# Early blocks split one block sooner, their low parts on VectorE, and row operations of the groups in another order

## The reference

```python
s = jnp.einsum('bhpd,phnd->bhpn', q, sub_keys).astype(jnp.float32)
top_s, top_i = lax.top_k(s, PEER_TOPK)
...
eid = e1 * PEER_NKEYS + e2
gate = jax.nn.softmax(best_s, axis=-1)
u_sel = expert_u[eid]
act = jax.nn.gelu(jnp.einsum('bd,bhkd->bhk', xb, u_sel).astype(jnp.float32), approximate=False)
v_sel = expert_v[eid]
return jnp.einsum('bhk,bhkd->bd', (gate * act).astype(xb.dtype), v_sel)
```

## Time and profile before

| | us |
|---|---|
| median of 3 runs | 3806.78 |
| lowest and highest | 3801.97, 3807.18 |
| the profiled execution, its own time | 3811.23 |
| its span | 3809.5 |
| PE busy | 3467.4 (91%) |
| DVE busy | 2623.9 (69%) |
| ACT busy | 1017.8 (27%) |
| POOL busy | 1063.9 (28%) |
| mean granted TensorE clock, share of full | 0.95 |

### The profile page before, as it was taken

One profiled execution on the slowest core, in us unless ns is written; L12 is line 12 of the kernel. 1 busy time (PEld: TensorE's weight loads), 2 busy tenths in 40 slices (PEclk: granted clock), 3 DMA queues, 4 the chain that ended last, 5 costly groups with the idle time before them and its releaser, 6 DMA issues.

```text
span 3809.5 us, 57302 instructions
## 1 busy us (share of the span) xinstructions
PE 3467.4 (91%) x21552; PEld 3385.4 (89%) x21552; DVE 2623.9 (69%) x4889; ACT 1017.8 (27%) x1345; POOL 1063.9 (28%) x809
## 2 busy tenths in 40 slices
PE   6989999899998999886888799999999999999997
PEld 6989999699998999885777789999999999999996
DVE  5553434223443499997666788888888888888886
ACT  5732222111322232222333222222222222222222
POOL 0000000000000233221111545555455555544551
PEclk8999999699999999997888999999999999999998
DMA  2111111111322233224655989888888888888983
GB/s 100 39 36 37 35 44 44 50 44 45 135 84 73 93 116 106 88 92 127 190 180 180 347 309 323 297 301 307 295 312 322 317 300 308 309 307 311 323 307 106
DMA packets 304485, 699.11 MB, mean 184 GB/s; under 512 B 23872, under 2 KB 124224, under 8 KB 303328
## 3 DMA queue, kind: packets, MB, share of 16 engines
q0 software_dynamic: 98736, 363.50, 26.3%
q1 hardware_dynamic: 104112, 276.89, 21.4%
q10 hardware_dynamic: 101504, 56.89, 4.9%
HBM read 604.96 MB, written 92.22 MB: 183 GB/s over the span
## 4 chain that ended last, share of the span: by engine, by line
PE 64%; DVE 22%; DMA 6%; issue 4%; ACT 2%; POOL 1%; DVEq 1%; ACTq 0%; SPq 0%; PEldq 0%; POOLq 0%
PE PS L1420 21%; PE PS L358 15%; PE PS L1135 6%; PE PS L1403 5%; PE PS L1164 5%; PE PS L1343 5%; DMA SLOT<-rows_u,EID 4%; DVE XLF L1927 3%; PE PS L1382 3%; DVE SLOT L1918 2%; POOL WL L674 1%; PE PS L373 1%; DVE VL L1911 1%; DVE besti L1775 1%; DVE sc L1766 1%
## 5 line engine op out<-in xcount | busy, mean ns | idle before, releaser
L1420 PE MATMUL PS<-AH,VH 128*128 128x368 f32 x2048 | 523.0, 337 | 90.7 <-DVE VL L1911 76.9
L1420 PE MATMUL PS<-AH,VL 128*128 128x368 f32 x2048 | 517.5, 334 | 0.0
L1420 PE MATMUL PS<-AL,VH 128*128 128x368 f32 x2048 | 516.9, 334 | 0.0
L1420 PEld LDWEIGHTS PS<-AH,VH 128*128 128x128 f32 x2048 | 368.8, 191 | 102.1 <-DVE VL L1911 87.0
L704 POOL DMA_INDIRECT SLOT<-rows_u,EID x256 | 334.3, 1306 | 384.2 <-DVE XLF L1927 304.0
L704 POOL DMA_INDIRECT SLOT<-rows_v,EID x256 | 362.9, 1417 | 247.3 <-DVE SLOT L1918 214.9
L1420 PEld LDWEIGHTS PS<-AL,VH 128*128 128x128 f32 x2048 | 371.5, 191 | 0.0
L1420 PEld LDWEIGHTS PS<-AH,VL 128*128 128x128 f32 x2048 | 371.2, 191 | 0.0
L1998 DVE TENSOR_TENSOR HID<-HID,PS 128x736 f32<-128x736 f32 x256 | 235.4, 919 | 177.4 <-PE PS L1420 162.8
L1343 PE MATMUL PS<-XH,WH 128*128 128x368 f32 x1024 | 278.6, 352 | 80.2 <-POOL WL L674 80.2
L674 POOL TENSOR_TENSOR WL<-RAW,WH 128x1024 fp32r<-128x1024 f32 x64 | 172.2, 2692 | 628.5 <-ACT WH L947 628.5
(11 more groups left out here) (327 smaller groups left out, 6741.8 us busy)
## 6 DMA issues: line engine op xcount, KB each, us to landing
RAW<-experts_u SPq DMA_DIRECT2D x128, 512.0 KB, 3.7
VRAW<-experts_v SPq DMA_DIRECT2D x256, 256.0 KB
gate_matrices<-stg ACTq DMA_DIRECT2D x22, 2048.0 KB, 8.8
GW<-gate_matrices SPq DMA_DIRECT2D x96, 384.0 KB
RAW<-weights SPq DMA_DIRECT2D x69, 512.0 KB, 3.5
activations<-AS SPq DMA_DIRECT2D x64, 368.0 KB, 2.5
AS<-activations SPq DMA_DIRECT2D x64, 368.0 KB
GW<-gate_matrices SPq DMA_DIRECT2D x32, 320.0 KB
```

The source lines that it names most:

```text
L1420: mm = pe.matmul(PS[:, 4 + 2 * (d % 2) + t, 0:CH], w[:, d % 2, c * P:c * P + P], x[:, c, t * CH:t * CH + CH], start=(c == 0 and n == 0), s ...
```

## The change

Three things, in two stages.

1. `SEL_E` gives the sixth and the ninth tile five blocks instead of four. So `E0` is 46 instead of 44, and 18 blocks instead of 20 are left to the gate-matrix stage.
2. In the gate-matrix stage ACT splits two blocks ahead (after the gelu of block m it splits m+2; block `E0+1` is split ahead of the stage), and VectorE makes the low parts, between its own operations, three steps after the step in which the block's slot came free (`e_end`). GpSimd has no work there.
3. In the groups TensorE's order of slices 0 and 1 changes, so that slice 0 ends one chunk sooner, and VectorE's row operations are placed elsewhere: two fewer ahead of the first `HID` addition, one more at d = 3 and one more at d = 6 (which had none left before).

```diff
-SEL_E = (5, 5, 5, 5, 5, 4, 5, 4, 4)
+SEL_E = (5, 5, 5, 5, 5, 5, 5, 4, 5)
...
+        def e_end(m):
+
+            return min(s for s in range(NSTEP) if e_steps(s)[1] >= len(STEPS) * (m - E0 + 1))
...
                 for r in range(2, SEL_E[i] + 1):
                     e_low(FIRST_E[i] + r, (FIRST_E[i] + r) % 2)
-            for n in range(E0 + 1, NE):
-                e_low(n, n % 2)
...
+            e_split((E0 + 1) % 2, E0 + 2, 16 * ((E0 + 1) // 2 + 1))
             for s in range(NSTEP):
...
-                    e_block(m, m % 2, 16 * (m // 2 + 1), m + 1 < NE)
+                    e_block(m, m % 2, 16 * (m // 2 + 1), False)
+                    if m + 2 < NE:
+                        e_split(m % 2, m + 3, 16 * ((m + 2) // 2 + 1))
...
-                order = [(d, c) for cs in (range(GE - 1), (GE - 1,)) for d in range(2) for c in cs]
+                order = [(0, 0), (0, 1), (0, 2), (1, 0), (1, 1), (0, 3), (1, 2), (1, 3)]
...
                 ins.then_inc(w_hot, 1)
+                for m in range(E0 + 1, NE):
+                    if s == (e_end(m - 2) + 3 if m > E0 + 1 else 2):
+                        dve.wait_ge(e_lo, m)
+                        dve.wait_ge(e_hi, m + 1)
+                        dve.tensor_tensor(WL[:, m % 2, :], RAW[:, m % 2, :], WH[:, m % 2, :].bitcast(F32),
+                                          ALU.subtract).then_inc(e_lo, 1)
...
-                    for j in range(early[0], early[0] + n):
+                    for j in range(early[0], min(early[0] + n, SPR)):
                         sp_u(0, j, j)
-                    early[0] += n
+                        early[0] = j + 1
...
-                    between(2 if h == 0 else 3)
+                    between(2 if h == 0 else SPR if first else 1)
...
-                    some((3 if d < 4 else 2) if first else 2 if d in (2, 4) else 1)
+                    some((3 if d < 4 else 2) if first else 2 if d in (2, 3, 4) else 1 if d < 7 else 0)
```

## The result

The changed kernel takes 3598.34 us (median of 4 runs, 3596.05 to 3601.01), beside 3806.98 us for the kernel before on the same chip (4 runs, 3801.97 to 3808.2). The ratio is 0.9455, 95% interval 0.9438 to 0.9471. The profiled execution took 3599.17 us, against 3811.23.

The account below looks back on a forecast made before the run. The prediction saw no engine full in the gate-matrix stage, held up at block starts, and groups held up for `VL`. It summed 3811.2 - 109.5 + 1 - 79.8 - 2.4 = 3620.5, less 4.4, to 3616 us, 8 in 10 between 3602 and 3656.

Parts of the forecast that it names:

- What bounds the stage: Gate-matrix stage: VectorE becomes the longer engine, 245.2 us against TensorE's 237, without waits for low parts.
- a cover of some 7 us: Gate-matrix stage: VectorE's low part is ready some 7 us before TensorE needs it, so no wait there.
- Selection: Selection: two added blocks and their GpSimd low parts cost 0 to 4 us, taken as +1 us.
- the 4 us of both together: Selection: by the skill's rule on shared SBUF interfaces both added low parts delay VectorE, 4 us longer.
- Groups: Groups: the wait for `VL` goes, 51.50 to 48.75 us a group, -79.8 us over 29, and -2.4 us before them.
- sign of being wrong: Gate-matrix stage and groups: ACT waiting for stores (landings above 12 us), clock below 0.9, or PE waits at named places.
- The 3645 us of operations that run one after another at 0.69: Gate-matrix stage rival: VectorE's steps don't close up, 275 us, kernel 3645; with the store rival 15 in 100.
- half of the groups' wait: Groups rival: late gathers or `AL` keep half of the wait, 41 us, kernel 3657 us; 13 in 100.
- 245.2 + 2.5, say 248 us.: Gate-matrix stage: VectorE's work of 245.2 us plus 2.5 for the start, against 357.5, so -109.5 us.
- The start, 2.5 us.: Start of the gate-matrix stage: two or three TensorE steps at 1.2 GHz hold VectorE up by 2.5 us.
- With a rest of 0.1 us a group for jitter, a group takes 48.75.: Groups: 48.64 us for 288 matmuls without a wait, plus 0.1 for jitter, makes 48.75 us a group.
- Less 4.4.: Whole kernel: 4.4 us comes off the sum because the profiled execution, 3811.2, exceeded the runs' median of 3806.8.

Follow-up runs that it names:

- late_dve: Kernel after, but ACT splits as late as before, with VectorE making the low part one step after the block's end: 3664.69 us, ratio 0.9627.
- ahead_pool: Kernel after, still split two blocks ahead, but with the gate-matrix stage's low parts back on GpSimd: 3628.27 us, ratio 0.9522.
- sel_ahead: Kernel after, plus an earlier ACT split at the third block of each selection tile, ahead of the softmax's exponential: 3610.81 us, ratio 0.9487.
- gate_only: Kernel after with the groups' old chunk order and old row operations, keeping the selection and gate-matrix changes: 3695.72 us, ratio 0.9696.

## Why the prediction was right, and where it was wrong

Right, by its own steps:
- *What bounds the stage.* VectorE became the longer engine, TensorE's waits for the low part went, GpSimd is idle, the clock is at 0.99. The step on the lead ("a cover of some 7 us") holds: VectorE never waits for a split in the stage. late_dve and ahead_pool show that both halves of the edit are needed, the lead for 66 us of the kernel's time and the engine for 30.
- *Selection.* +1.6 us measured for +1, as the step says: of the two added low parts one met an operation of VectorE. It was `cand` and not `pick`, and it cost 1.6 us instead of 2.0; the 4 us of both together did not come. The searches that the prediction held against the rule of "two SBUF inputs" are no test of it, since their `MAX8` reads one tensor (`best<-sc`).
- *Groups.* The wait for `VL` goes, and the next in line (`AL`, a gather) do not come late from the second group on, with a DMA share of 0.91, where the earlier trace rows has 0.86. The chunk-by-chunk account of 1 us for the order and more for the row operations came out as waits of 0.60 and 2.4 us (with the 0.2 us of slack, 0.8 and 2.8 were forecast), and as 22.5 and 90.0 us of the kernel's time.
- *The rivals.* One sign of being wrong did show: ACT waits for stores, twice, 4.0 us in all, with a landing above 12 us. VectorE isn't held up by it, so this sign was no sign of a slower kernel; a landing above 12 us was there before, too. With a DMA share of 0.85, landings of the 2 MB stores in the kernel after are a little longer at the median than in the earlier trace rows:

```profile
DMA to landing us min/median/max: 8.8/10.2/12.6
```

  The 3645 us of operations that run one after another at 0.69 are 47 us too long; the starts stand 0.602 apart. The Trainium skill's words on the flush (VectorE: DVE Perf Modes, Terms) give it no length; to take a row's whole duration for it was the prediction's reading. Nor was half of the groups' wait kept. (The waits for gathers before, "up to 0.54", are up to 0.8 us in other groups, 8.7 us at 17 such places.)

Wrong: the time, by 17.7 us, and the low end of the range by 3.7. What failed is the size of two terms, the stage's 248 us and the group's 48.75, and not the mechanism: each was priced from its dear side. The terms, each with what it measured:
- *"245.2 + 2.5, say 248 us."* Measured 241.4. VectorE's steps close up at 0.602 us an operation, not 0.61 (2.9 us over 368); a low part takes 1.14 from start to start, not its row's duration of 1.22 (1.4 us over 17). I had taken start-to-start for the one and a duration for the other. Nor do TensorE's waits for `HOTG` come to "some 0.5 us a block"; they are 0.2 us at 12 places.
- *The start, 2.5 us.* It isn't there. The clock was 0.50 for the first 6 us as forecast, but TensorE has little to do in them: busy 3.24 of 6.00, and VectorE waited 0.2 us for it in the whole stage. "Two or three steps at 1.2 GHz hold VectorE up" was false: at that clock TensorE kept pace. The tail to the first late block gave 0.9 more.
- *"With a rest of 0.1 us a group for jitter, a group takes 48.75."* Measured 48.51. 48.64 was already read from a group with a wait in it, and the jitter is nil where TensorE never waits: 29 x (48.75 - 48.52) = 6.7 us.
- *"Less 4.4."* The profiled run of before lay 4.4 above its median. That of after lies 0.8 above its own, so 3.6 us too much came off, and 5.8 us came that no term had.

By these the stage is 7.5 us better than forecast, the groups 6.7 + 0.9 and the end 1.0, and the selection 0.6 worse: 15.5. The rest is 5.8 - 3.6 = 2.2 us, and the sum of both is the 17.7. The range failed with the sum: I gave 2 in 100 to less than 3603, "where jitter and start cost nothing and the selection gains". But jitter and start were margins that I had added myself, and no row showed their cost. To drop them alone would not have been enough: with 245.2 for 248 and 48.64 for 48.75 the sum is 3610. The paces had to be right too, and all three can be read in the trace of before, from start to start: 0.603 us an fp16 operation (median), 1.136 a low part in the groups, and 8.09 a block of 48 matmuls with 4.04 a slice of 24, which is 48.5 a group. With these the sum is 3602, the low end of the range as it was given. The last 3.7 us are small terms that no row of before showed; 2.2 of them are the 4.4, which stands for one execution.

## What to carry to other kernels

When a stage goes from waiting to full, price its operations from start to start in a stretch where they follow each other without a gap, not by their durations, and add a margin only where a row shows a wait. That sum, without a margin, belongs in the middle of the range and not at its low end: here it would have been 3602, and 3598 was measured. In this stage the lead of the producer was worth more than twice the faster engine, and each was priced alone by undoing the other. Before moving a GpSimd operation in time, look at what VectorE does at the new place: here one edit moved the collision from one operation to the next. And a GpSimd operation beside a VectorE that never pauses may stand until VectorE stops.

## What the runs showed of the hardware

- A GpSimd subtraction of 128x1024 fp32 and some operations of VectorE shut each other out. In the selection the one that starts second pays. Where the low part starts 0.78 us behind `hot` (2.29 us, unchanged), it is the low part that goes from 2.40 to 3.71 us; the bf16 `pick` right behind `hot` then goes from 1.23 to 3.2. `cand` (fp32, 128x128), which starts 0.64 us behind a low part of 2.40 us, goes from 0.27 to 1.9, and L1839 in sel_ahead, of the same shape, from 0.29 to 2.3. So it is no matter of 16 bits.
- Where VectorE runs without a gap, GpSimd may not get in at all: in ahead_pool four low parts of 14.3 to 15.0 us each ended 2.2 us behind VectorE's last operation, and VectorE kept its pace beside them. Where it did get in, an fp16 operation went from 0.69 to 2.9 us. The second of these I had expected, the first not.
- Not all operations meet so: beside the searches, the low part keeps its 2.40 us and they theirs. The reductions of `pick` did not lengthen (2285 to 2289 ns in all nine tiles).
- Durations and pace differ. VectorE's fp16 operations lasted 0.684 us (median) in the kernel after and 0.757 in gate_only; they start 0.602 apart in both, and the stage took 241.4 us in both.
- With a DMA share of 0.91 in the groups and 0.85 in the stage, VectorE waited 0.5 us for a gather, once, and TensorE never for a DMA; ACT waited 4.0 us for stores.
